# LayerNorm sums on one engine, conditioned values on ScalarE, and the last two channel groups regrouped, in a one-core streaming encoder layer

## The chip, the core and the metric
The kernel runs on one core of a Trainium2 chip. A core has five engines that run their own instruction streams and meet only at semaphores: TensorE (PE, matmuls; PEld is its weight load), VectorE (DVE), ScalarE (ACT), GpSimd (POOL) and SyncE (SP, which here only issues DMAs). The metric is the time of one execution in microseconds, given as the median of three runs.

## The reference, cut to what matters
One layer for 1,056 frames (1,024 of a prompt and 32 of a running stream, laid side by side), 1,024 channels:

```
out  = merged @ w_out                                # token-mixing sub-layer, before this: attention and mLSTM
x    = LayerNorm(alpha*x + gate1*out) * ln1_w + ln1_b          # the first LayerNorm, "LN1"
h    = x*(1+scale2) + shift2
u    = h @ w_up + b_up                               # 1024 -> 5632
uc   = conv_b + causal conv of width 3 over frames(u)
a, g = split(uc)                                     # 2816 each
x    = LayerNorm(alpha*x + gate2*((a*gelu(g)) @ w_down)) * ln2_w + ln2_b   # the second, "LN2"
```

All of it is float32. Each matmul operand is split into a rounded part (hi) and a remainder (lo), and three products (hi*hi, hi*lo, lo*hi) are summed, so that a 128 x 352 output tile over 1,024 channels takes 24 matmuls.

## The kernel before
Channels lie on the 128 partitions, in KT = 8 tiles (index m or k); frames lie along the free axis in NT = 3 blocks of 352 (index n). The third block holds the end of the prompt and the other stream, so an instruction with per-stream constants is issued in two pieces there (320 and 32). x lives in `x_c` (XC), the matmul input in `x_hilo_a` (XA).

Weights come as 512 KB panels, in one list whose order `ffn_panels()` writes out. SP loads them into two buffers; POOL splits each into hi and lo (`split`, L366 a cast and L368 a subtraction) and puts it into a ring of three slots (`w_hilo`). A panel may be written when the panel three places ahead of it in the ring has been used up by PE. The last panels have a place of their own (`w_tail_hilo`).

PE works through PSUM banks, eight of them, in an order that `bank_fills()` writes out and that PE's code repeats: a `fill` waits until the bank's former tile has been read.

The stages that the change touches:

- **LN1.** For each block n, PE makes the eight tiles of `merged @ w_out` (`out_tile`, L668). DVE adds each into x (`out_take`, L1467). Two running sums over the eight tiles are kept in `ln_sums`: the plain sum by POOL (`ln_sum`, L377), and the sum of squares, squared by ACT (L1089) and added by DVE (`ln_add_square`, L1476). After the third tile of the next block PE multiplies both sums by a matrix of 1/1024 (`ln_means`, L677 and L680, which wait for the semaphores of the two sums). DVE and ACT make the variance, its root and the shift (`ln_var`, `ln_sqrt`, `ln_shift`), and DVE normalises two tiles at a time (`ln_pair`, L1494 and L1496). Then h of each tile is made twice: rounded by ACT (`h2_high`, L1104) and in full by DVE (`h2_value`, L1502); POOL subtracts (`h2_low`, L385). PE's first up projection of a block waits for `h2_low`.
- **The channel sub-layer.** 11 groups j (FG = FF = 11). Each has four up panels ("u", j, 0..3), with three 24-matmul tiles each (`up`, L691), and two down panels ("d", j, 0..1), with twelve 6-matmul tiles each (`down`, L701). ACT moves an up tile out of PSUM (`up_take`, L1114) and begins the convolution (`up_tap`, L1121); DVE adds the two other taps (`conv_first` L1543, `conv_second` L1546); ACT takes the gelu (L1125), DVE multiplies (`ffn_prod`, L1556), ACT rounds (`ffn_round`, L1130), DVE makes the remainder (`ffn_low`, L1561 and L1562). PE runs the down tiles of group j-1 between the up tiles of group j, and DVE adds them into x (`down_take`, L1569).
- **The last groups.** The second half of the third last group's down tiles (FG-3, m = 4..7) comes after the up tiles of the last group. The last two groups have no down tiles of their own: for each (m, n) their products are summed in one bank (`down_last`, key "t", twelve matmuls), n by n.
- **LN2.** As LN1, on the "t" tiles; DVE takes a tile, adds a square, and normalises pairs of the block before; ACT scales pairs (L1175) and SP stores them. Behind the last tile stand both sums, PE's two means, the variance, the root, four pairs and the last store.

## Time and profile before
| | us |
|---|---|
| median of 3 runs (lowest, highest) | 2039.43 (2037.89, 2040.49) |
| profiled execution: its own time | 2039.05 |
| profiled execution: span from first to last instruction | 2037.2 |
| PE busy | 1946.1 (96%) |
| DVE busy | 1062.0 (52%) |
| ACT busy | 604.4 (30%) |
| POOL busy | 592.1 (29%) |

Between 1265 and 1903 us PE has no idle time at all; the stages above lie at 1121 to 1265 us (LN1 and the first up tiles) and at 1903 us to the end (the last groups and LN2). In a row of the timeline the first number is the start, the second the time from there to the end of the last instruction of the row, "xN" their count, and the bracket at the end the idle time of that engine just before and what ended it.

### The profile page before, as it was taken

To read this page: it belongs to the slowest core of one execution; us is meant where nothing else is said; L and a number is where in the kernel's file an instruction comes from. 1 tells how busy PE (TensorE), PEld (TensorE's weight loads), DVE (VectorE), ACT (ScalarE), POOL (GpSimd) and SP (SyncE) were. 2 spreads that over 40 slices of the span, in tenths; PEclk is the share of its full clock that TensorE was granted. 3 is DMA by queue.
4 is the path that set the end of the run, shared out by engine and by line. 5 is a ranking of instruction groups with operands and counts; after the bars stand their busy time and mean duration, and the time that the engine had idled before them with its cause. 6 is when DMAs were issued, how large, how long until landed. Compare 5 with 4: busy or idle time off the path is not lost.

```text
span 2037.2 us, 29596 instructions
## 1 busy us (share of the span) xinstructions
PE 1946.1 (96%) x11919; PEld 1845.6 (91%) x11919; DVE 1062.0 (52%) x1907; ACT 604.4 (30%) x1377; POOL 592.1 (29%) x354
## 2 busy tenths in 40 slices
PE   8889999999999999999899999999999999999983
PEld 6889888888799999989899998999999999999982
DVE  2797454344543333554434399554445445554577
ACT  1102444444223232333311134322222222322323
POOL 2332111121222222222233764323233332323321
PEclk9999999999999999999999999999999999999986
DMA  7562111111223332225533300111111111111102
GB/s 306 205 197 89 65 48 58 43 64 43 86 84 126 98 123 95 95 90 190 179 120 127 98 11 32 43 51 42 52 42 52 42 52 43 43 51 42 53 11 77
DMA packets 74183, 171.39 MB, mean 84 GB/s; under 512 B 8496, under 2 KB 37680, under 8 KB 73920
## 3 DMA queue, kind: packets, MB, share of 16 engines
q1 hardware_dynamic: 27168, 91.50, 13.3%
q10 hardware_dynamic: 46880, 78.02, 11.4%
q8 instruction: 94, 1.54, 0.3%
q14 instruction: 41, 0.34, 0.1%
HBM read 137.27 MB, written 32.22 MB: 83 GB/s over the span
## 4 chain that ended last, share of the span: by engine, by line
PE 82%; DVE 11%; DVEq 2%; ACT 2%; issue 1%; ACTq 1%; DMA 1%; POOL 0%; POOLq 0%
PE acc L421 30%; PE px L691 16%; PE acc L691 9%; PE px L701 7%; PE acc L701 4%; DVE adaT_tmp L1236 4%; PE px L484 2%; PE px L505 2%; PE px L503 2%; PE px L446 2%; PE px L668 1%; DVE x_c L1496 1%; DVE ln_sums L1476 1%; PE px L585 1%; DVEq L1495 1%
## 5 line engine op out<-in xcount | busy, mean ns | idle before, releaser
L421 PE MATMUL acc<-x_hilo_a,w_hilo 128*128 128x352 f32 x4176 | 727.5, 329 | 20.7 <-ACT x_c L799 10.0
L421 PEld LDWEIGHTS acc<-x_hilo_a,w_hilo 128*128 128x128 f32 x4176 | 674.3, 190 | 39.6 <-issue 28.9
L366 POOL CAST w_hilo<-w_raw 128x1024 fp32r<-128x1024 f32 x134 | 147.6, 1101 | 1299.2 <-PE acc L421 785.5
L368 POOL TENSOR_TENSOR w_hilo<-w_raw,w_hilo 128x1024 fp32r<-128x1024 f32 x134 | 343.5, 2563 | 10.7
L691 PE MATMUL px<-x_hilo_a,w_hilo 128*128 128x352 f32 x2016 | 326.9, 322 | 0.0
L691 PEld LDWEIGHTS px<-x_hilo_a,w_hilo 128*128 128x128 f32 x2016 | 323.0, 188 | 0.5 <-issue 0.5
L691 PE MATMUL acc<-x_hilo_a,w_hilo 128*128 128x352 f32 x1152 | 186.4, 321 | 0.0
L691 PEld LDWEIGHTS acc<-x_hilo_a,w_hilo 128*128 128x128 f32 x1152 | 183.8, 188 | 0.0
L701 PE MATMUL px<-ffn_act,w_hilo 128*128 128x352 f32 x888 | 151.0, 323 | 0.0
L701 PEld LDWEIGHTS px<-ffn_act,w_hilo 128*128 128x128 f32 x888 | 144.1, 189 | 0.2
L1569 DVE SCALAR_TENSOR_TENSOR x_c<-px,mod,x_c 128x352 f32<-128x352 f32 (+1 forms) x198 | 87.9, 483 | 68.6 <-PE px L701 68.4
L1114 ACT ACTIVATE u_rows<-px,ffn_consts 128x352 f32<-128x352 f32 (+2 forms) x113 | 50.7, 477 | 221.8 <-PE px L691 221.8
L1540 DVE COPY conv_out<-u_rows 128x2 f32<-128x2 f32 x44 | 16.1, 365 | 157.2 <-ACTq L1119 157.1
L1236 DVE CUSTOM_DVE_ANT_0 adaT_tmp<-adaT_ring,silu_bc 128x1024 f32<-128x1024 f32 x64 | 93.8, 1503 | 5.1 <-issue 4.2
L1543 DVE SCALAR_TENSOR_TENSOR stage<-u_rows,ffn_consts,stage 128x1058 f32<-128x1058 f32 x44 | 85.1, 1933 | 21.3 <-ACT stage L1121 21.3
L701 PE MATMUL acc<-ffn_act,w_hilo 128*128 128x352 f32 x552 | 95.7, 324 | 0.0
L868 ACT ACTIVATE stage<-acc 128x352 f32<-128x352 f32 x123 | 54.9, 457 | 129.6 <-PE acc L421 112.6
L701 PEld LDWEIGHTS acc<-ffn_act,w_hilo 128*128 128x128 f32 x552 | 90.0, 190 | 0.5 <-issue 0.5
L1569 DVE SCALAR_TENSOR_TENSOR x_c<-acc,mod,x_c 128x352 f32<-128x352 f32 (+2 forms) x122 | 55.0, 486 | 62.2 <-PE acc L701 62.0
L421 PE MATMUL acc<-x_hilo_b,w_hilo 128*128 128x352 f32 x504 | 80.4, 321 | 0.5 <-DVE stage L1453 0.5
L421 PEld LDWEIGHTS acc<-x_hilo_b,w_hilo 128*128 128x128 f32 x504 | 80.1, 188 | 0.7 <-issue 0.7
L1114 ACT ACTIVATE u_rows<-acc,ffn_consts 128x352 f32<-128x352 f32 (+2 forms) x63 | 28.8, 482 | 158.4 <-PE acc L691 158.4
(227 smaller groups left out, 2319.3 us busy)
## 6 DMA issues: line engine op xcount, KB each, us to landing
w_raw<-in_w_panels SPq DMA_DIRECT2D x142, 512.0 KB, 3.7
z_spill<-stage ACTq DMA_DIRECT2D x41, 528.0 KB, 2.7
adaT_ring<-in_w_adaT ACTq DMA_DIRECT2D x32, 512.0 KB, 4.4
stage<-z_spill ACTq DMA_DIRECT2D x20, 528.0 KB, 4.6
ada_ring<-in_w_ada SPq DMA_DIRECT2D x16, 512.0 KB, 9.4
zc<-z_spill ACTq DMA_DIRECT2D x8, 1024.0 KB, 7.6
x_c<-in_x SPq DMA_DIRECT2D x8, 528.0 KB, 10.2
x_c<-in_x ACTq DMA_DIRECT2D x8, 528.0 KB, 3.8
```

Source lines behind the costliest of these rows:

```text
L366: nc.gpsimd.tensor_copy(to[:, 0, :], raw[:, s, :]).then_inc(w_hi, 1)
L368: nc.gpsimd.tensor_tensor(to[:, 1, :], raw[:, s, :], to[:, 0, :].bitcast(F32), ALU.subtract).then_inc(w_ready, 1)
L421: last = mm(acc[:, n, 0:NW], whl[:, slot, wi, k * P:(k + 1) * P], rhs[:, xi, k, n * NW:(n + 1) * NW], start=(k == 0 and j == 0), stop=(k = ...
L446: last = mm(px[0:2, 3, i * P:(i + 1) * P], silu[:, 1, k, :], ada[:, q % KT, k * P:(k + 1) * P], start=(k == 0), stop=(k == KT - 1))
L484: last = mm(px[:, j // 2, (j % 2) * BAND:(j % 2) * BAND + w], qs[:, par, 4 * g + j, :], ks[:, par, g, 0:w], start=True, stop=True, skip_gr ...
L691: last = mm(to, w[:, wi, k * P:(k + 1) * P], XA[:, xi, k, n * NW:(n + 1) * NW], start=(k == 0 and q == 0), stop=(k == KT - 1 and q == 2))
L701: done = mm(to, w[:, wi, col:col + P], act[:, xi, k, n * NW:(n + 1) * NW], start=(first and k == 0 and q == 0), stop=(last and k == 1 and ...
L868: A(ST[:, slot, n * NW:(n + 1) * NW], acc[:, n, 0:NW], ACT.Copy).then_inc(acc_free[n], 1)
L1114: last = A(ub[:, i, 2 + a + 2 * s:2 + b + 2 * s], src[:, a - n * NW:b - n * NW], ACT.Identity, bias=fc[:, j, i, 0:1])
L1236: V.tensor_tensor_reduce(adaT_tmp[:, s, :], adaT[:, i, :], sbc[:, s, :], 1.0, 0.0, ALU.mult, ALU.add, ast[:, i, s:s + 1])
L1543: V.scalar_tensor_tensor(ST[:, i, 0:CW], ub[:, i, 0:CW], fc[:, j, i, 1:2], ST[:, i, 0:CW], ALU.mult, ALU.add)
L1569: last = V.scalar_tensor_tensor(XC[:, m, a:b], src[:, a - n * NW:b - n * NW], mod[:, 5, m, s:s + 1], XC[:, m, a:b], ALU.mult, ALU.add)
```

## The change
1. The plain sums move from POOL to DVE: `ln_add` follows each `out_take` and each "t" take. POOL's `ln_sum` is gone.
2. h in full is made by ACT, just before the rounded one (`h2_high` now issues both); DVE's `h2_value` is gone.
3. The split of the third up panel, which stood behind the second sum of the last block, now stands behind the eight `h2_low` of the first block.
4. The third last group's down tiles all run inside the loop; the up tiles of the last group follow without down tiles among them; then come the "t" tiles. In block n = 0 PE first opens all eight banks and runs the six matmuls of group FG-2 for all m, then the six of group FG-1 for all m. Blocks 1 and 2 are as before. One panel instead of two has its own place.
5. Small reorderings: both gelus ahead of both roundings in ACT's code (so far gelu, rounding, gelu, rounding), both products ahead of both remainders in DVE's; the signal for the conv state's store comes after the last remainder.

```
-    last = order.pop()
-    order += [("u", FF - 1, i) for i in range(4)]
-    return order + [last] + [("d", j, s) for j in (FF - 2, FF - 1) for s in range(2)]
+    order += [("u", j, i) for j in range(FF - TAIL + 1, FF) for i in range(4)]
+    return order + [("d", j, s) for j in range(FF - TAIL, FF) for s in range(2)]
...
-            for m in range(1, KT):
-                ln_sum(0, m, 0)
-            for n in range(1, NT):
-                for m in range(1, KT):
-                    ln_sum(0, m, n)
-                    if m == 2 and n == NT - 1:
-                        split(P_FFN + 2)
-                    if 3 <= m < KT - 1:
-                        for k in (2 * m - 6, 2 * m - 5):
-                            h2_low(n - 1, k)
-            for k in range(KT):
-                h2_low(NT - 1, k)
+            for n in range(NT):
+                for k in range(KT):
+                    h2_low(n, k)
+                if n == 0:
+                    split(P_FFN + 2)
...
-            for m in range(4, KT):
-                for n in range(NT):
-                    down(FG - 3, m, n)
-            for n in range(NT):
+            open_banks = [fill(("t", m, 0)) for m in range(KT)]
+            for m in range(KT):
+                down_last(open_banks[m], m, 0, range(FG - TAIL, FG - 1))
+            for m in range(KT):
+                down_last(open_banks[m], m, 0, range(FG - 1, FG))
+            for n in range(1, NT):
                 for m in range(KT):
-                    down_last(m, n)
+                    down_last(fill(("t", m, n)), m, n, range(FG - TAIL, FG))
...
             def h2_high(n, k):
+                q = n * KT + k
                 act.wait_ge(ln_t, n * KT // 2 + k // 2 + 1)
+                wait(act, h2_lo, q - 5)
+                for a, b, s in pieces(n):
+                    A(hslot(q)[:, a - n * NW:b - n * NW], XC[:, k, a:b], ACT.Identity, scale=der[:, s, k:k + 1],
+                      bias=der[:, 2 + s, k:k + 1])
...
+            def ln_add(ln, m, n):
+                cols = slice(n * NW, (n + 1) * NW)
+                V.tensor_tensor(lsum[:, 0, cols], XC[:, 0, cols] if m == 1 else lsum[:, 0, cols], XC[:, m, cols], ALU.add).then_inc(s1_add, 1)
...
                     down_take(("t", m, n))
+                    if m:
+                        ln_add(1, m, n)
                     if m > 1:
                         ln_add_square(1, m - 1, n)
```

One middle tile of LN1 on DVE (block 1, m = 4), before:

```order
L1467 SCALAR_TENSOR_TENSOR x_c<-px,mod,x_c 128x352
L1476 TENSOR_TENSOR ln_sums<-ln_sums,stage 128x352
L1494 TENSOR_TENSOR x_c<-x_c,ln_rstd 128x2x352
L1496 TENSOR_TENSOR x_c<-x_c,ln_shift 128x2x352
L1502 TENSOR_SCALAR stage<-x_c,der 128x352 x2
```

The same tile now (take, plain sum, sum of squares, pair):

```order
L1453 SCALAR_TENSOR_TENSOR x_c<-px,mod,x_c 128x352
L1486 TENSOR_TENSOR ln_sums<-ln_sums,x_c 128x352
L1462 TENSOR_TENSOR ln_sums<-ln_sums,stage 128x352
L1480 TENSOR_TENSOR x_c<-x_c,ln_rstd 128x2x352
L1482 TENSOR_TENSOR x_c<-x_c,ln_shift 128x2x352
```

The two values of h have left DVE, and one sum has come in between the take and the sum of squares.

POOL in LN1, from the end of block 1 to the middle of block 2, before (L377 is the plain sum, L385 `h2_low`, L366 and L368 the split of the third up panel):

```order
L385 TENSOR_TENSOR x_hilo_a<-stage,x_hilo_a 128x352 x2
L377 TENSOR_TENSOR ln_sums<-ln_sums,x_c 128x352
L377 TENSOR_TENSOR ln_sums<-x_c 128x352
L377 TENSOR_TENSOR ln_sums<-ln_sums,x_c 128x352
L366 CAST w_hilo<-w_raw 128x1024
L368 TENSOR_TENSOR w_hilo<-w_raw,w_hilo 128x1024
L377 TENSOR_TENSOR ln_sums<-ln_sums,x_c 128x352
```

All of POOL's work in LN1 now:

```order
L375 TENSOR_TENSOR x_hilo_a<-stage,x_hilo_a 128x352 x8
L365 CAST w_hilo<-w_raw 128x1024
L367 TENSOR_TENSOR w_hilo<-w_raw,w_hilo 128x1024
L375 TENSOR_TENSOR x_hilo_a<-stage,x_hilo_a 128x352 x16
```

Only remainders of h and one split are left; the split comes at once after the eighth remainder of block 0.

PE from the last up tiles on, before (L691 up tiles, L701 down tiles; acc and px are PSUM banks):

```order
L691 MATMUL px<-x_hilo_a,w_hilo 128x352 x72
L701 MATMUL px<-ffn_act,w_hilo 128x352 x12
L701 MATMUL acc<-ffn_act,w_hilo 128x352 x18
L701 MATMUL px<-ffn_act,w_hilo 128x352 x30
L701 MATMUL acc<-ffn_act,w_hilo 128x352 x18
L701 MATMUL acc<-ffn_act_tail,w_tail_hilo 128x352 x6
L701 MATMUL px<-ffn_act,w_hilo 128x352 x6
```

PE from the last up tiles on, now (L670 up tiles, L680 down tiles):

```order
L670 MATMUL acc<-x_hilo_a,w_hilo 128x352 x48
L680 MATMUL acc<-ffn_act,w_hilo 128x352 x6
L680 MATMUL px<-ffn_act,w_hilo 128x352 x30
L680 MATMUL acc<-ffn_act,w_hilo 128x352 x12
L680 MATMUL acc<-ffn_act_tail,w_hilo 128x352 x6
L680 MATMUL px<-ffn_act_tail,w_hilo 128x352 x18
L680 MATMUL px<-ffn_act_tail,w_tail_hilo 128x352 x12
L680 MATMUL acc<-ffn_act_tail,w_tail_hilo 128x352 x12
```

Before, 78 matmuls (72 of group FG-3 and the first 6 of FG-2) stood between the last up tile and the first use of the last group's activations (`ffn_act_tail`); now 48 do, all of group FG-2.

## Rows read from the trace of the kernel before
**Rows 1.** Who waited for whom, PE: total us, times, longest.
```profile
PE px L677 <- POOL ln_sums L377: 25.6, 4, 12.0
```
**Rows 2.** Timeline of LN1 around the two means with a wait, PE and DVE.
```profile
1197.02 0.83 PE L677 MATMUL px<-ln_sums,ones 128*128 128x352 f32 x2 [1.80 <-POOL ln_sums L377]
...
1224.08 0.70 DVE L1467 SCALAR_TENSOR_TENSOR x_c<-px,mod,x_c 128x320 f32<-128x320 f32 x2
...
1227.14 1.51 PE L677 MATMUL px<-ln_sums,ones 128*128 128x352 f32 x2 [5.80 <-POOL ln_sums L377]
...
1229.11 5.99 PE L691 MATMUL px<-x_hilo_a,w_hilo 128*128 128x352 f32 x24
```
**Rows 3.** Timeline of LN1, one tile (block 1, m = 4), DVE and POOL.
```profile
1178.23 0.58 DVE L1467 SCALAR_TENSOR_TENSOR x_c<-px,mod,x_c 128x352 f32<-128x352 f32 x1
...
1178.95 0.56 DVE L1476 TENSOR_TENSOR ln_sums<-ln_sums,stage 128x352 f32<-128x352 f32 x1
1179.43 1.63 DVE L1494 TENSOR_TENSOR x_c<-x_c,ln_rstd 128x704 f32<-128x704 f32 x1
1180.27 1.59 POOL L377 TENSOR_TENSOR ln_sums<-ln_sums,x_c 128x352 f32<-128x352 f32 x1
...
1182.70 0.84 DVE L1502 TENSOR_SCALAR stage<-x_c,der 128x352 f32<-128x352 f32 x2
```
**Rows 4.** Timeline of LN1, ACT: rounded h, two tiles each, blocks 0 and 2.
```profile
1177.07 1.26 ACT L1104 ACTIVATE x_hilo_a<-x_c,der 128x352 fp32r<-128x352 f32 x2 [3.29 <-DVE x_c L1496]
...
1236.40 1.81 ACT L1104 ACTIVATE x_hilo_a<-x_c,der 128x320 fp32r<-128x320 f32 x4 [2.00 <-DVE x_c L1496]
```
**Rows 5.** Chain of work that ended last: start, us, 72 matmuls at full clock.
```profile
1903.39 11.45 PE acc L691 x72
```
**Rows 6.** Timeline from the last up tile to the first use of its activations.
```profile
1926.32 0.71 ACT L1114 ACTIVATE u_rows<-px,ffn_consts 128x320 f32<-128x320 f32 x2 [3.26 <-PE px L691]
...
1928.44 2.62 DVE L1543 SCALAR_TENSOR_TENSOR stage<-u_rows,ffn_consts,stage 128x1058 f32<-128x1058 f32 x1 [0.90 <-ACT stage L1121]
...
1932.05 2.39 POOL L368 TENSOR_TENSOR w_tail_hilo<-w_raw,w_tail_hilo 128x1024 fp32r<-128x1024 f32 x1
...
1932.76 2.80 DVE L1546 SCALAR_TENSOR_TENSOR stage<-u_rows,ffn_consts,stage 128x1058 f32<-128x1058 f32 x1
...
1937.31 2.73 DVE L1556 TENSOR_TENSOR stage<-stage 128x1058 f32<-128x1058 f32 x1
...
1942.26 1.26 DVE L1556 TENSOR_TENSOR stage<-stage 128x1058 f32<-128x1058 f32 x1 [0.62 <-ACT stage L1125]
...
1943.56 1.06 ACT L1130 ACTIVATE ffn_act_tail<-stage 128x1024 fp32r<-128x1024 f32 x1 [1.33 <-DVE stage L1556]
...
1946.27 1.22 DVE L1561 TENSOR_TENSOR ffn_act_tail<-stage,ffn_act_tail 128x1024 fp32r<-128x1024 f32 x1
...
1947.64 2.12 PE L701 MATMUL acc<-ffn_act_tail,w_tail_hilo 128*128 128x352 f32 x6 [8.93 <-DVE ffn_act_tail L1562]
```
**Rows 7.** Timeline of LN2, DVE: block 1's start, block 2's end.
```profile
1967.65 0.53 DVE L1476 TENSOR_TENSOR ln_sums<-ln_sums,stage 128x352 f32<-128x352 f32 x1
...
1970.54 0.58 DVE L1569 SCALAR_TENSOR_TENSOR x_c<-px,mod,x_c 128x352 f32<-128x352 f32 x1 [1.32 <-PE px L701]
...
2012.63 0.70 DVE L1569 SCALAR_TENSOR_TENSOR x_c<-px,mod,x_c 128x320 f32<-128x320 f32 x2
2013.47 1.30 DVE L1476 TENSOR_TENSOR ln_sums<-ln_sums,stage 128x352 f32<-128x352 f32 x1
2014.69 0.88 DVE L1494 TENSOR_TENSOR x_c<-x_c,ln_rstd 128x704 f32<-128x704 f32 x1
...
2016.45 0.71 DVE L1569 SCALAR_TENSOR_TENSOR x_c<-px,mod,x_c 128x320 f32<-128x320 f32 x2
...
2021.14 0.52 DVE L1481 TENSOR_TENSOR ln_var<-px,ln_rstd 128x352 f32<-128x352 f32 x1 [1.94 <-PE px L680]
```
**Rows 8.** Stretches: us, PE, PEld, DVE, ACT, POOL busy (count), PEclk, DMA.
```profile
1947.60:1953.00 5.40, 5.36 (x18) 5.36 (x19) 0.58 (x1) 0.50 (x1) 0.00 (x0) 0.50 0.00 0
```

More of the change, by code:

```diff
@@ L60 @@
 NSLOT = 3
+TAIL = 2
 def ffn_panels():
     order = [("u", 0, i) for i in range(4)]
-    for j in range(1, FF - 1):
+    for j in range(1, FF - TAIL + 1):
         order += [("u", j, 0), ("u", j, 1), ("d", j - 1, 0), ("u", j, 2), ("u", j, 3), ("d", j - 1, 1)]
-    last = order.pop()
-    order += [("u", FF - 1, i) for i in range(4)]
-    return order + [last] + [("d", j, s) for j in (FF - 2, FF - 1) for s in range(2)]
+    order += [("u", j, i) for j in range(FF - TAIL + 1, FF) for i in range(4)]
+    return order + [("d", j, s) for j in range(FF - TAIL, FF) for s in range(2)]
 PANEL = {key: P_FFN + q for q, key in enumerate(ffn_panels())}
@@ L75 @@
 WO_PANELS = range(P_OUT + 2, P_OUT + KT)
-TAIL_PANELS = range(N_PANEL - 2, N_PANEL)
+TAIL_PANELS = range(N_PANEL - 2 * TAIL + NSLOT, N_PANEL)
 RING = [p for p in range(N_PANEL) if p not in WO_PANELS and p not in TAIL_PANELS]
@@ L95, in bank_fills @@
             order += [("u", j, i, n) for i in (2 * h, 2 * h + 1) for n in range(NT)]
-            if 2 * j + h < 2 * FF - 3:
+            if j <= FF - TAIL:
                 order += [("d", j - 1, m, n) for m in range(4 * h, 4 * h + 4) for n in range(NT)]
-    order += [("d", FF - 3, m, n) for m in range(4, KT) for n in range(NT)]
     for n in range(NT):
@@ L370, in split @@
                 pool.sem_inc(raw_used, 1)
-            def ln_sum(ln, m, n):
-                pool.wait_ge(r_rdy, rank(ln, m, n) + 1)
-                done = (KT - 1) * (NT * ln + n) + m - 1
-                wait(pool, s1_add, done)
-                cols = slice(n * NW, (n + 1) * NW)
-                nc.gpsimd.tensor_tensor(lsum[:, 0, cols], XC[:, 0, cols] if m == 1 else lsum[:, 0, cols], XC[:, m, cols], ALU.add)\
-                  .then_inc(s1_add, 1)
             def h2_low(n, k):
@@ L711, in down, with down_last @@
                 down_part(to, j, m, n, True, True).then_inc(ready(("d", j, m, n))[0], 1)
-            def down_last(m, n):
-                to = fill(("t", m, n))
-                for j in (FG - 2, FG - 1):
+            def down_last(to, m, n, groups):
+                for j in groups:
                     if n == 0 and m == 0:
@@ L719, in down_last @@
                         pe.wait_ge(w_ready, PANEL["d", j, m // 4] + 1)
-                    done = down_part(to, j, m, n, j == FG - 2, j == FG - 1)
-                done.then_inc(ready(("t", m, n))[0], 1)
+                    done = down_part(to, j, m, n, j == FG - TAIL, j == FG - 1)
+                if groups[-1] == FG - 1:
+                    done.then_inc(ready(("t", m, n))[0], 1)
             first = [fill(("o", 0, n)) for n in range(NT)]
@@ L757, in _ @@
                                 down(j - 1, m, n)
-            for m in range(4, KT):
-                for n in range(NT):
-                    down(FG - 3, m, n)
-            for n in range(NT):
+            open_banks = [fill(("t", m, 0)) for m in range(KT)]
[4 more added lines that the diff above has]
+            for n in range(1, NT):
                 for m in range(KT):
-                    down_last(m, n)
-                    if m == 2 and n:
+                    down_last(fill(("t", m, n)), m, n, range(FG - TAIL, FG))
+                    if m == 2:
                         ln_means(1, n - 1)
@@ L1496, in ln_pair @@
                 V.tensor_tensor(pair, pair, ln_c[:, n % 2:n % 2 + 1, :].to_broadcast([P, 2, NW]), ALU.add).then_inc(ln_t, 1)
-            def h2_value(n, k):
-                q = n * KT + k
-                wait(dve, h2_lo, q - 5)
-                for a, b, s in pieces(n):
-                    last = V.tensor_scalar(hslot(q)[:, a - n * NW:b - n * NW], XC[:, k, a:b], der[:, s, k:k + 1],
-                                           der[:, 2 + s, k:k + 1], ALU.mult, ALU.add)
-                last.then_inc(h2_d, 1)
-            def h2_pair(n, k):
-                ln_pair(n, k)
-                dve.drain()
-                h2_value(n, k)
-                h2_value(n, k + 1)
+            def ln_add(ln, m, n):
+                cols = slice(n * NW, (n + 1) * NW)
+                V.tensor_tensor(lsum[:, 0, cols], XC[:, 0, cols] if m == 1 else lsum[:, 0, cols], XC[:, m, cols], ALU.add).then_inc(s1_add, 1)
             for n in range(NT):
@@ L1531, in _ @@
             for k in range(0, KT, 2):
-                h2_pair(2, k)
+                ln_pair(2, k)
             dve.wait_ge(h2_hi, NT * KT)
-            dve.wait_ge(h2_d, NT * KT)
+            dve.drain()
             for k in range(KT):
@@ L1585, in _ @@
                 ffn_prod(0, t)
+            for t in range(2):
                 ffn_low(0, t)
-            for j in range(1, FG - 1):
+            for j in range(1, FG - TAIL + 1):
                 ffn_conv(j, 0)
```

47 lines of the change are left out of this document (16 added, 31 removed).

## The prediction
> **What bounds the kernel now.** I read the list of who waited for whom first, for PE. PE is busy 96% of the span, so only the places where it waits, and the work behind its last matmul, can give time back. The largest entry after the start of the kernel is the mean of LN1 and LN2, held up by POOL's plain sum: 25.6 us in four waits [rows 1]. Then the timeline around each. In LN1 the two waits are 1.80 and 5.80 us [rows 2], and nothing but DVE's pace is behind them: DVE's last take of block 2 starts at 1224.08, while PE had been done long before. The third place is the last group: 8.93 us for its activations [rows 6]. After that DVE sets the pace to the end: the longest of the four waits, 12.0, is PE's at the very last mean [rows 1]. So there are three stages to price: LN1, the last group, LN2.
>
> The reason for DVE's pace stands in rows 3 and 7. A sum of squares (L1476) takes 0.53 us when POOL is idle and 1.30 when POOL's sum starts beside it [rows 7]; the first half of a pair (L1494) takes 0.88 alone [rows 7] and 1.63 beside POOL [rows 3]; POOL's sum itself is stretched to 1.59 beside DVE [rows 3]. The stretch is each time about what the other needed. So a POOL instruction and a DVE instruction that reads two operands from SBUF run one after the other, and POOL's sum costs DVE about 0.78 us (1.30 less 0.53). The Trainium skill (SBUF — State Buffer, "Who interferes with whom") says the same as a rule: with two SBUF inputs VectorE takes the pair of ports that it shares with GpSimd, and whoever comes first keeps it for the whole instruction. It makes the price of a POOL sum the whole of POOL's instruction, not a share; these rows agree.
>
> **LN1.** Removed from DVE per tile in the steady part (m = 4 to 6): two values of h, 0.84, and POOL's plain sum as a neighbour, 0.78. Added: one sum, 0.48 from one start to the next (L1476 to L1494 in rows 3). But two POOL subtractions per tile remain, and now they begin later. Before, the cycle of a tile is 5.2 us (1178.23 to 1182.70 plus 0.84, rows 3). Now: take 0.72 (1178.23 to 1178.95), two sums 0.48 each: 1.7. POOL's first subtraction is released by two ACT activations (1.26, rows 4), so at about 1.4; it gets in after the second sum and, at some 0.85, holds DVE to 2.5. First half of the pair to 3.4; the second subtraction, released at 2.6, gets in next, to 4.2; second half to 5.0 at most, the next take a little before: I take 4.8. That saves 0.4 per tile, three times per block. In the tile m = 3, which has no subtraction beside it, the saving is 0.84 + 0.78 - 0.48 = 1.1. Together 2.3 per block. With a small gain in the tile before, I take 2.4, so the last take of block 2 starts near 1221.7.
>
> Block 1's saving does not carry into block 2: the moved split now falls on block 2's first sums, and a split's subtraction is 2.39 long [rows 6]; before, it lay beside the reciprocal, which POOL did not disturb. The wait of 1.80 goes, but DVE enters block 2's tile m = 3 as late as before.
>
> After the last take of block 2 (0.83 with two pieces) the plain sum is done at +1.3. The sum of squares is now later than the plain sum: ACT has four activations for the last pair (2 x 1.26) ahead of its square (0.5), and a subtraction of POOL and the addition follow: +4.1. PE resumes the up tiles at 1221.7 + 4.1 + 0.5 = 1226.3 instead of 1229.11: **2.8 us earlier**.
>
> Block 2 of h must then keep up. ACT's two tiles take 1.81 before [rows 4], 3.62 now. From the first up tile after the means, the first pair begins at +7.3 (1236.40 less 1229.11, rows 2 and 4), four pairs add 14.5, three evictions between them about 1.4 (estimated at one activation of 0.45 each), POOL about 1: +24.2. PE needs the last at five tiles of 3.82 (a third of rows 5), 2.2 more for the first at half clock (5.99, rows 2), and 7/8 of a tile: +24.6. It just fits; were the clock full, PE would gain 2.2 and wait 1.8. Bounds of LN1: if the two subtractions and ACT's doubled work keep the old cycle and h is late, a loss of 1; if neither holds DVE, a gain of 5 (cycle 3.7, all of the first wait).
>
> **The last group.** 72 down matmuls move ahead of the last up tiles: these end 11.45 us later [rows 5]. From ACT's eviction of the last up tile to PE's use of the activations it was 21.3 us (1926.32 to 1947.64, rows 6). In between DVE had twelve takes of the third last group, and POOL three splits; now no take, and two splits. By rows 6, from the eviction: first tap's start at +2.1 and its end at +4.7 as before, beside the first split; then the cast of the second split (about 0.9) and the second tap (1.1 of its 2.80, the rest was blocking): +6.8. The second split's subtraction gets in next (2.39): +9.2, then the first product (1.1): +10.3; second product, 1.2 more: +11.5; its rounding 1.2 (1943.56 to the start of its last small piece and that piece): +12.7; the two remainders 1.37 each, the second behind the first: **+14.1**. So PE resumes 11.45 - 7.2 = 4.25 later than now. PE's cover is shorter, 48 matmuls (7.6 us) behind the wait for eight free banks (until the last eviction is over, 0.71), so it still idles about 6 us and still starts at half clock, 0.50 granted after the wait [rows 8], 2.12 for the first six matmuls [rows 6].
>
> The rule of the skill speaks against the change here, since the two splits that are left fall on the convolution of the last group alone. That is in the 14.1; without any blocking the same chain is 10.1 (2.1 + 1.3 + 1.4 + 1.3 + 1.3 + 1.2 + 1.5), and with none of the blocking gone and only the takes gone (12 at some 0.4) 16.4.
>
> **LN2, counted from PE's resumption.** Nothing is left on POOL here, so no sum is blocked. Block 0: before, each tile took PE twelve matmuls, 1.91, and block 1's first take came at 1966.94 (0.71 before the first of rows 7), 19.3 after the resumption. Now half of these matmuls are done before, and DVE sets the pace: first take at +2.1, then two tiles at half-clock pace (about 1.8 each), and tiles of take 0.71 and two sums 0.44 each, 1.6: block 0 ends at +15.1, **4.2 saved**. Blocks 1 and 2, up to the last take at 2016.45 [rows 7], 49.5 us: eleven of thirteen sums of squares were blocked and lose 0.78 each (-8.6; the cycle of 3.82 from 2012.63 to 2016.45 holds one), thirteen plain sums come in at 0.44 (+5.7), and the waits for PE at the block's start go, one of them 1.32 [rows 7]: **3.9 saved**. From the last take to the variance it was 4.69 (2016.45 to 2021.14): the plain sum no longer waits for POOL, and PE's first mean starts earlier: **0.5 saved**. Behind it nothing changes.
>
> **The sum.** LN1 -2.8, last group +4.25, LN2 -4.2 - 3.9 - 0.5: -7.1. The profiled execution took 2039.05 (span 2037.2 and 1.85 around it), so 2031.9; the median of before, 0.38 higher, would give 2032.3. I forecast **2032**. At nothing I cost the reordering of gelus, products and remainders in groups 0 to 9: PE has no idle time there, and a group's remainders are needed some 30 us after its last up tile, behind the next group's two up panels.
>
> **Rivals.**
> - *LN1 gives nothing back.* ACT and POOL's subtractions become the pace where POOL's sums were: 5.80 stays. For it: only 0.4 per tile was found. Against: 0.84 per tile leaves DVE for certain. Then 2039.05 - 4.3 = 2034.7 (2034 to 2036.5).
> - *The cover is lost and eats the gain.* The chain of the last group stays at 21.3, each DVE step waiting for POOL and ACT as before, so PE resumes 11.45 later instead of 4.25: 2032 + 7.2 = 2039 (2036.5 to 2043). For it: two splits start just when the last up tile ends. Against: one split and twelve takes are gone, and the takes stand in rows 6 as the gaps between the taps and the products.
> - *DVE is the bound and gets more work: slower.* If 1.30 were the own price of a sum of squares in LN2 (waiting for ACT's square, not for POOL), no blocking would go, and 0.44 per added sum would stand alone: in blocks 1 and 2 +5.7 less the 1.8 of waits, block 0 about +1, the last group +4.25, LN1 -1.4 (0.48 - 0.84 per tile): +7.6, so 2047. It decides from the point where L1476 in LN2 stays above 0.9. Against: the same instruction takes 0.53 where POOL rests.
> - *More than forecast.* The last group's chain at 10.1: 2028.
>
> **How the numbers follow.** A median of three tells 0.2% (4.1 us) from no change: faster means under 2035.4, slower over 2043.5. Chances: forecast (2028.5 to 2035.4) 0.54; LN1 gives nothing 0.18, half of it under 2035.4; cover lost 0.15, 0.13 of it within 0.2% and 0.01 beyond either end; slower 0.07; more 0.06. Faster 0.54 + 0.09 + 0.06 + 0.01 = 0.70, slower 0.08, same 0.22. The range leaves out a tenth on either side: 2026.5 at the lower end (LN1's bound of 5 or the chain at 10.1, and a little of the other), 2037.5 at the upper (LN1 at nothing and the chain at 16.4 give 2037).
>
> **What would show it.** In the profile after: L1476's successor (sum of squares) at 0.53 in all of LN2 and the plain sum at the same; the DVE cycle of a tile in LN1 4.8, in LN2 3.4; PE's wait at the first mean of LN1 gone, at the second about 3.6 before the plain mean and 2 before the squares; PE's wait for the last group's activations about 6, ended 14 us after the last up tile's eviction; last take 60 to 61 us after that. Wrong: a sum of squares over 0.9 in LN2, an LN1 cycle of 5.2 or more, a wait of PE for `h2_low` in block 2 over 2 us, or a chain of 16 us and more behind the last up tile.

## The result

The changed kernel takes 2030.07 us, the median of six runs (2028.93 to 2031.47); the kernel before, timed beside it, 2039.96 (2037.77 to 2045.10). The ratio is 0.9950, with a 95% interval of 0.9937 to 0.9963: about 10 us faster, more than twice the 0.2% (4.1 us) that the prediction took as what can be told from no change. The profiled execution took 2029.85 us, its span 2028.1. DVE's busy time hardly moved (1062.0 to 1056.2 us), POOL's fell by 39 and ACT's rose by 17.

Who PE waited for now (total us, times, longest):

```profile
PE px L656 <- DVE ln_sums L1486: 19.6, 3, 11.0
...
PE acc L680 <- DVE ffn_act_tail L1539: 5.0, 1, 5.0
...
PE px L659 <- DVE ln_sums L1462: 1.7, 1, 1.7
...
```

The mean's 25.6 us in four waits [rows 1] are 19.6 in three, and it is DVE's own sum (L1486) that ends them; the 8.93 for the last group's activations [rows 6] are 5.0. The new entry of 1.7 is the wait for the sum of squares that was foreseen.

The timeline of PE at LN1's means in the changed kernel (start, us, bracket: wait before and releaser):

```profile
1194.79 0.75 PE L656 MATMUL px<-ln_sums,ones 128*128 128x352 f32 x2
...
1222.13 0.83 PE L656 MATMUL px<-ln_sums,ones 128*128 128x352 f32 x2 [2.80 <-DVE ln_sums L1486]
...
1224.66 1.51 PE L659 MATMUL px<-ln_sums,ones 128*128 128x352 f32 x2 [1.70 <-DVE ln_sums L1462]
...
1225.45 5.32 PE L670 MATMUL px<-x_hilo_a,w_hilo 128*128 128x352 f32 x24
```

The first wait is gone and the second is 4.5 in two parts where it was 5.80; the up tile behind it starts 3.66 earlier than in [rows 2], of which 0.29 was there before LN1 began (its first out tile started at 1120.67 instead of 1120.96). One tile of LN1 (block 1, m = 5) and the moved split, DVE and POOL, same timeline:

```profile
1181.20 0.57 DVE L1453 SCALAR_TENSOR_TENSOR x_c<-acc,mod,x_c 128x352 f32<-128x352 f32 x1
...
1181.91 0.53 DVE L1486 TENSOR_TENSOR ln_sums<-ln_sums,x_c 128x352 f32<-128x352 f32 x1
1182.36 0.52 DVE L1462 TENSOR_TENSOR ln_sums<-ln_sums,stage 128x352 f32<-128x352 f32 x1
...
1182.65 2.60 POOL L375 TENSOR_TENSOR x_hilo_a<-stage,x_hilo_a 128x352 fp32r<-128x352 f32 x2 [2.12 <-ACT x_hilo_a L1090]
1182.79 1.64 DVE L1480 TENSOR_TENSOR x_c<-x_c,ln_rstd 128x704 f32<-128x704 f32 x1
...
1184.51 1.48 DVE L1482 TENSOR_TENSOR x_c<-x_c,ln_shift 128x704 f32<-128x704 f32 x1
...
1185.92 0.57 DVE L1453 SCALAR_TENSOR_TENSOR x_c<-acc,mod,x_c 128x352 f32<-128x352 f32 x1
...
1195.73 2.39 POOL L367 TENSOR_TENSOR w_hilo<-w_raw,w_hilo 128x1024 fp32r<-128x1024 f32 x1
...
1195.90 2.60 DVE L1486 TENSOR_TENSOR ln_sums<-ln_sums,x_c 128x352 f32<-128x352 f32 x1
```

From take to take it is 4.72, as against 5.2 in [rows 3]. An instruction is called blocked here when it takes longer than alone because the other engine is at work. Both halves of the pair are still blocked (1.64 and 1.48, alone 0.88 and 0.89), now both by POOL's subtractions; before, the first half was behind a subtraction (POOL's L385, from 1178.09 on, two in 2.22) and the second behind the plain sum, which starts at 1180.27 [rows 3]. The last two rows are the split on block 2's first sums: a sum of 0.53 takes 2.60.

The last group in the changed kernel, ACT, DVE, POOL and PE, answering to [rows 6]:

```profile
1933.47 0.71 ACT L1100 ACTIVATE u_rows<-acc,ffn_consts 128x320 f32<-128x320 f32 x2 [3.26 <-PE acc L670]
...
1935.60 2.63 DVE L1520 SCALAR_TENSOR_TENSOR stage<-u_rows,ffn_consts,stage 128x1058 f32<-128x1058 f32 x1 [0.90 <-ACT stage L1107]
...
1937.34 1.79 POOL L365 CAST w_tail_hilo<-w_raw 128x1024 fp32r<-128x1024 f32 x1 [0.23 <-POOL w_hilo L367]
1938.30 1.94 DVE L1523 SCALAR_TENSOR_TENSOR stage<-u_rows,ffn_consts,stage 128x1058 f32<-128x1058 f32 x1
1939.21 3.30 POOL L367 TENSOR_TENSOR w_tail_hilo<-w_raw,w_tail_hilo 128x1024 fp32r<-128x1024 f32 x1
1940.17 4.64 DVE L1533 TENSOR_TENSOR stage<-stage 128x1058 f32<-128x1058 f32 x2
...
1947.49 2.13 PE L680 MATMUL acc<-ffn_act_tail,w_hilo 128*128 128x352 f32 x6 [4.99 <-DVE ffn_act_tail L1539]
```

From the eviction to PE's resumption it is 14.02 where it was 21.32, and PE resumes at almost the same moment as before. LN2, DVE, grouped by form from 1940 us on (count | busy us, mean ns of one), answering to the sums of [rows 7]:

```profile
L1462 DVE TENSOR_TENSOR ln_sums<-ln_sums,stage 128x352 f32<-128x352 f32 x21 | 10.9, 520 | 0.4
L1486 DVE TENSOR_TENSOR ln_sums<-ln_sums,x_c 128x352 f32<-128x352 f32 x18 | 9.5, 526 | 2.4
```

And its ends in the timeline, DVE: block 1's first take, the last two takes and the variance.

```profile
1962.14 0.58 DVE L1546 SCALAR_TENSOR_TENSOR x_c<-acc,mod,x_c 128x352 f32<-128x352 f32 x1
...
2004.52 0.70 DVE L1546 SCALAR_TENSOR_TENSOR x_c<-px,mod,x_c 128x320 f32<-128x320 f32 x2
...
2008.00 0.70 DVE L1546 SCALAR_TENSOR_TENSOR x_c<-px,mod,x_c 128x320 f32<-128x320 f32 x2
...
2012.31 0.53 DVE L1467 TENSOR_TENSOR ln_var<-px,ln_rstd 128x352 f32<-128x352 f32 x1 [1.89 <-PE px L659]
```

All 21 sums of squares are at 0.52, a tile takes 3.48 (2004.52 to 2008.00; 3.82 before), block 1 begins 14.65 after PE's resumption (19.3 before), the last take comes 60.51 after it (68.81 before).

### The profile page after: what moved, and what is told of

Read it like the earlier page. It is cut to its first block, busy times and chain, and to the rows that moved or that the text cites. A ratio compares the mean times of both kernels' runs of the same rounds, so it can differ in the third digit from the quotient of the medians.

```text
span 2028.1 us, 29540 instructions
## 1 busy us (share of the span) xinstructions
PE 1944.3 (96%) x11919; PEld 1843.8 (91%) x11919; DVE 1056.2 (52%) x1917; ACT 621.4 (31%) x1409; POOL 552.8 (27%) x312
## 4 chain that ended last, share of the span: by engine, by line
PE 83%; DVE 10%; ACT 2%; DVEq 2%; issue 1%; ACTq 1%; DMA 1%
PE acc L400 30%; PE px L670 15%; PE acc L670 9%; PE px L680 6%; DVE adaT_tmp L1222 4%; PE acc L680 4%; PE px L647 2%; PE px L463 2%; PE px L484 2%; PE px L482 2%; PE px L425 2%; PE acc L647 1%; PE px L564 1%; PE px L566 1%; PE px L565 1%
## 5 line engine op out<-in xcount | busy, mean ns | idle before, releaser
L367 POOL TENSOR_TENSOR w_hilo<-w_raw,w_hilo 128x1024 fp32r<-128x1024 f32 x135 | 349.1, 2586 | 10.8
L670 PE MATMUL px<-x_hilo_a,w_hilo 128*128 128x352 f32 x1992 | 322.5, 322 | 0.0
L670 PEld LDWEIGHTS px<-x_hilo_a,w_hilo 128*128 128x128 f32 x1992 | 318.6, 188 | 0.5 <-issue 0.5
L670 PE MATMUL acc<-x_hilo_a,w_hilo 128*128 128x352 f32 x1176 | 190.4, 321 | 0.0
L670 PEld LDWEIGHTS acc<-x_hilo_a,w_hilo 128*128 128x128 f32 x1176 | 187.6, 188 | 0.0
L680 PE MATMUL px<-ffn_act,w_hilo 128*128 128x352 f32 x894 | 150.5, 322 | 0.0
L680 PEld LDWEIGHTS px<-ffn_act,w_hilo 128*128 128x128 f32 x894 | 144.1, 188 | 0.2
L680 PE MATMUL acc<-ffn_act,w_hilo 128*128 128x352 f32 x546 | 94.4, 324 | 1.1 <-ACT u_rows L1100 1.1
L680 PEld LDWEIGHTS acc<-ffn_act,w_hilo 128*128 128x128 f32 x546 | 88.6, 189 | 1.9 <-issue 1.9
```

The costliest lines, as they stand in the source:

```text
L367: nc.gpsimd.tensor_tensor(to[:, 1, :], raw[:, s, :], to[:, 0, :].bitcast(F32), ALU.subtract).then_inc(w_ready, 1)
L670: last = mm(to, w[:, wi, k * P:(k + 1) * P], XA[:, xi, k, n * NW:(n + 1) * NW], start=(k == 0 and q == 0), stop=(k == KT - 1 and q == 2))
L680: done = mm(to, w[:, wi, col:col + P], act[:, xi, k, n * NW:(n + 1) * NW], start=(first and k == 0 and q == 0), stop=(last and k == 1 and ...
```

## The experiments

The time of one kernel scatters by some 3 us either way; its stages scatter less. So every run is read by three stretches of its profile. **A**: from the first out tile to the up tile behind LN1's second mean. **B**: from there to PE's resumption with the last group's activations. **C**: from there to PE's last mean of a plain sum. Each is a difference of two starts in PE's timeline. The kernel before has A 108.15, B 718.53, C 70.71; the changed kernel 104.78, 722.04, 62.02. Four kernels that leave LN1 as in the changed kernel have A within 104.79 to 104.82. But two that leave it as before have 108.15 and 108.39, and two that make h on ACT and the plain sums on POOL have 103.06 and 104.01, though LN1's second mean starts equally late in them, 102.06 and 102.05 after the first out tile (in the other pair it differs by 0.25). Here are these means, first h on ACT, then "mixed" (PE):

```profile
1222.58 0.83 PE L676 MATMUL px<-ln_sums,ones 128*128 128x352 f32 x2 [3.42 <-POOL ln_sums L377]
```

```profile
1222.18 1.51 PE L672 MATMUL px<-ln_sums,ones 128*128 128x352 f32 x2 [3.40 <-POOL ln_sums L377]
```

Behind the same wait one mean ran at 0.83 and the other at 1.51; the granted clock was 0.88 over the 2.5 us from 1222 in the first, 0.50 over the 3 us from 1222 in the second. So A holds up to 1 us of PE's clock behind its wait, and a difference in A of less than that is read only together with the start of the mean. Between runs the first out tile itself starts anywhere from 1119.5 to 1124.2, in stages that no kernel here touches. That adds to the scatter of the times; how much of it this is, and its cause, were not looked for. Each ratio in the table is to the kernel before timed beside that run (medians 2038.20 to 2041.48), so medians of different rows are compared by their ratios.

| kernel | median us (n) | ratio to before | A | B | C |
|---|---|---|---|---|---|
| sums on VectorE alone | 2038.36 (10) | 0.9989 (0.9979 to 0.9999) | 111.08 | 718.02 | 66.54 |
| h on ScalarE alone | 2033.88 (10) | 0.9973 (0.9963 to 0.9982) | 103.06 | 718.36 | 71.06 |
| both | 2031.04 (4) | 0.9953 (0.9939 to 0.9968) | 104.79 | 717.96 | 67.58 |
| last groups alone | 2038.22 (10) | 0.9991 (0.9978 to 1.0004) | 108.39 | 722.24 | 63.04 |
| changed, POOL reads in LN2 | 2047.24 (4) | 1.0044 (1.0031 to 1.0058) | 104.82 | 722.29 | 77.72 |
| changed, POOL writes in LN2 | 2030.30 (4) | 0.9960 (0.9947 to 0.9974) | 104.79 | 722.04 | 62.03 |
| changed, tail split late | 2029.71 (5) | 0.9956 (0.9944 to 0.9969) | 104.82 | 720.62 | 61.37 |
| changed, up split late | 2031.40 (5) | 0.9956 (0.9942 to 0.9970) | 103.08 | 723.42 | 62.59 |
| three edits | 2023.46 (4) | 0.9915 (0.9898 to 0.9932) | 101.56 | 720.06 | 60.86 |
| mixed, tail split late | 2025.63 (5) | 0.9936 (0.9923 to 0.9950) | 104.01 | 719.80 | 61.35 |

### The parts one by one

**The sums on VectorE alone** (part 1 of the change, on the kernel before):

```
-                    ln_sum(0, m, n)              # POOL, and the same for LN2
...
                     out_take(m, n)
+                    ln_add(0, m, n)              # DVE, and the same behind the "t" takes
```

> The kernel before with the plain LayerNorm sums alone moved from POOL to DVE (values of h stay on DVE, the last groups as before). Theory (a POOL instruction and a DVE instruction with two SBUF operands run one after the other; POOL's sum costs DVE 0.78 us, the sum on DVE 0.44): every sum of squares in LN2 takes 0.53 instead of 1.30; blocks 1 and 2 of LN2 3 us shorter, block 0 unchanged because PE's twelve matmuls per tile set its pace, the end 0.4 shorter, LN1 about 1 shorter (tile cycle 5.0 instead of 5.2). Together -4.5 us. Rival (the gain came from the regrouping, and sums on DVE only add work): +6 us or more, with the sum of squares still near 1.3.

Measured: about 2 us less in the medians, not 4.5. C fell by 4.2, a little more than foreseen (3.4), but A rose by 2.9 where a gain of 1 was expected. The sums are worth something in LN2 and cost in LN1. Where, the timeline of this kernel shows, from a tile of block 1 (m = 6) to behind LN1's first mean (DVE, POOL, PE):

```profile
1191.50 1.26 DVE L1461 TENSOR_TENSOR ln_sums<-ln_sums,stage 128x352 f32<-128x352 f32 x1
...
1198.83 2.50 POOL L368 TENSOR_TENSOR w_hilo<-w_raw,w_hilo 128x1024 fp32r<-128x1024 f32 x1
1199.05 2.66 DVE L1461 TENSOR_TENSOR ln_sums<-ln_sums,stage 128x352 f32<-128x352 f32 x1
...
1201.85 1.51 PE L665 MATMUL px<-ln_sums,ones 128*128 128x352 f32 x2 [3.83 <-DVE ln_sums L1461]
...
1202.64 6.69 PE L653 MATMUL px<-x_hilo_a,w_out_hilo 128*128 128x352 f32 x24
...
1209.44 0.71 DVE L1452 SCALAR_TENSOR_TENSOR x_c<-px,mod,x_c 128x320 f32<-128x320 f32 x2 [2.36 <-PE px L653]
```

POOL, without its sums, reaches the split early, and the split falls on the sum for which the mean waits. The wait goes on to cost clock: the out tile behind it takes 6.69 where it took 4.26 before (granted 0.58 from 1202 to 1209, and 1.00 from 1198 to 1202.2 before), and DVE then waits 2.36 for that tile. So this take comes 4.4 later after the first out tile than before (86.3 and 81.9); the tiles behind it win 1.4 back by the mean. In the tile itself only the sum of squares is blocked (1.26); the two halves of the pair take 0.88 and 0.89, where both were blocked before. With the sum that DVE now makes itself, the tile takes 5.08, as against 5.2.

**The values of h on ScalarE alone** (part 2):

```
             def h2_high(n, k):
+                for a, b, s in pieces(n):
+                    A(hslot(q)[:, a - n * NW:b - n * NW], XC[:, k, a:b], ACT.Identity, scale=der[:, s, k:k + 1], ...
...
-                h2_value(n, k); h2_value(n, k + 1)      # DVE, behind each pair
```

> The kernel before with the full values of h alone made by ACT. Theory: DVE loses 0.84 per tile in LN1, but POOL's three instructions per tile (two subtractions, one sum) and DVE's three (sum of squares, two halves of a pair) still take turns, 3 x 0.85 + 2.3 and the take: cycle stays at 5.0 to 5.4, so LN1 gains 0 to 1 us, LN2 nothing: -0.5 us in all. Rival (DVE's own work sets LN1's pace): cycle 4.4, LN1 2.5 to 3 us shorter by this part alone.

Measured: A fell by 5.1, so the rival held, and by more than it said. Of the 5.1, 4.1 are there when the second mean starts (106.18 after the first out tile before, 102.06 here); the last 1.0 is PE's clock, since the two means ran at 1.51 and 1.38 before and at 0.83 and 0.76 here. One tile of LN1 in this kernel (block 1, m = 6), DVE and POOL:

```profile
1184.35 0.57 DVE L1471 SCALAR_TENSOR_TENSOR x_c<-acc,mod,x_c 128x352 f32<-128x352 f32 x1
...
1185.06 0.56 DVE L1480 TENSOR_TENSOR ln_sums<-ln_sums,stage 128x352 f32<-128x352 f32 x1
1185.20 1.23 POOL L377 TENSOR_TENSOR ln_sums<-ln_sums,x_c 128x352 f32<-128x352 f32 x1
1185.55 1.63 DVE L1498 TENSOR_TENSOR x_c<-x_c,ln_rstd 128x704 f32<-128x704 f32 x1
...
1186.39 3.16 POOL L384 TENSOR_TENSOR x_hilo_a<-stage,x_hilo_a 128x352 fp32r<-128x352 f32 x2
...
1187.25 1.48 DVE L1500 TENSOR_TENSOR x_c<-x_c,ln_shift 128x704 f32<-128x704 f32 x1
1188.66 0.57 DVE L1471 SCALAR_TENSOR_TENSOR x_c<-acc,mod,x_c 128x352 f32<-128x352 f32 x1
```

The tile takes 4.31. POOL has three instructions in it here, two in the changed kernel and three before, and DVE has two blocked instructions (0.75 and 0.6 too long) in all three. So beside h on ACT a POOL sum less did not spare DVE a blocked instruction, while with h still on DVE, in the run above, it spared one; POOL's third instruction finds room beside DVE's takes, which read PSUM and are not blocked (0.57 beside POOL). What is left of the difference between 4.31 and 4.72 is the sum that DVE makes itself, 0.44.

**Both, with the last groups as before:**

> The kernel before with both moves, the last groups as before. Theory: LN1 as in the changed kernel (up tile after the second mean 3.7 us earlier, the half-clock tile 0.6 shorter: -4.3 in all), the last group as before, LN2 shorter by 3 in blocks 1 and 2 and 0.4 at the end: -7.6 us, 1.5 to 2 short of the changed kernel. Rival (the regrouping brings the gain of LN2): -4.3 us, LN2 as long as before.

Measured: A 104.79, as in the changed kernel, so the sums take back 1.7 of what h alone had, or 0.8 by the A of the mixed kernel; C 3.1 less than before. What they take back is not at the plain mean, which starts 0.6 earlier than with h alone (101.47 and 102.06 after the first out tile), but at the mean of the squares, which waits 1.70 more. In total 9.4 us between the medians, and 7.1 by the three stretches, near the theory's 7.6. So in the whole change the regrouped last groups bring some 1.5 by the stretches (B 4.1 more, C 5.6 less), which the ratios (0.9953 and 0.9950) can't tell.

**The last groups alone** (parts 4 and 5, with sums and h as before):

```
-            for m in range(4, KT):
-                for n in range(NT):
-                    down(FG - 3, m, n)
+            open_banks = [fill(("t", m, 0)) for m in range(KT)]
+            ...                                   # FG-2 for all m, then FG-1 for all m
```

> The changed kernel with the sums back on POOL and the values of h back on DVE, so only the regrouped last groups and the small reorderings are left. Theory: PE resumes 4.25 us later after the last group; LN2's block 0 is no longer paced by PE but by DVE with blocked sums (0.71 + 1.24 per tile, 1.95): 2.8 us back, and the waits for PE at block 1's start go, 1.8: -0.4 us in all, no change that can be told. Rival (regrouping brings LN2's gain): -4 us or better.

Measured: B rose by 3.7, C fell by 7.7, 3.7 less over all three stretches, so it was the rival (-4) that held in LN2, and not the -0.4. The medians differ by 2.25, which the scatter of this kernel (2033.83 to 2045.77) doesn't let one tell from no change. The fall in C is larger than the 4.2 of block 0 in the prediction; POOL's sums are still there, yet block 0 is no slower for them. Timeline of this kernel, DVE and POOL, in block 0 of LN2:

```profile
1955.55 0.53 DVE L1479 TENSOR_TENSOR ln_sums<-ln_sums,stage 128x352 f32<-128x352 f32 x1
1955.67 7.16 POOL L377 TENSOR_TENSOR ln_sums<-ln_sums,x_c 128x352 f32<-128x352 f32 x6
```

Here DVE's sum comes first and POOL's waits: six POOL sums take 1.19 each, at DVE's pace, and DVE's stay at 0.53 to 0.57. In blocks 1 and 2, up to the last take, ten of DVE's sums are at 1.30 to 1.32, as many as before. In the kernel before POOL is idle when a take ends, starts its sum at once and comes first, and DVE pays 1.30 [rows 7]. So the price of a POOL sum is not a constant; it goes to the engine that comes second.

### The contention by itself

**A POOL instruction that reads, put back beside each sum of LN2:**

```
+            for n in range(NT):
+                for m in range(1, KT):
+                    pool.wait_ge(r_rdy, rank(1, m, n) + 1)
+                    wait(pool, dm, n * (KT - 1) + m - 1)
+                    nc.gpsimd.tensor_tensor(ST[:, 2, 0:NW], ST[:, 0, 0:NW], ST[:, 1, 0:NW], ALU.add).then_inc(dm, 1)
```

> The changed kernel, with one idle instruction per tile put back on POOL in LN2: beside each take of a last tile (m = 1 to 7) POOL adds two 352-wide SBUF tiles into a third that nobody uses. Nothing waits for it, so only contention can act. Theory (a POOL instruction that reads SBUF and a DVE instruction with two SBUF operands take turns): the plain sum or the sum of squares beside it goes from 0.53 us to about 1.3; 21 of them, about 14 of these in blocks 1 and 2 where DVE sets the pace: LN2 8 to 14 us longer, 2040 against 2030. Rival (the 1.30 of before was the wait for POOL's result or for ScalarE's square): every sum stays at 0.53 and the time within 1 us of the changed kernel.

Measured: C rose by 15.7 to 77.72, beyond the upper end of 14. DVE and POOL by form from 1940 us on:

```profile
L1493 DVE TENSOR_TENSOR ln_sums<-ln_sums,x_c 128x352 f32<-128x352 f32 x18 | 23.5, 1307 | 2.5
L1469 DVE TENSOR_TENSOR ln_sums<-ln_sums,stage 128x352 f32<-128x352 f32 x21 | 10.8, 514 | 0.4
```

```profile
L392 POOL TENSOR_TENSOR stage<-stage 128x352 f32<-128x352 f32 x21 | 19.7, 936 | 62.5 <-DVEq L1557 62.5
```

The plain sum that starts beside it takes 1.31 instead of 0.53, all 21 of them (the three that begin a block stand in a row of their own, at 1.30): 21 x 0.78 = 16.4. Block 0, which the expectation had spared, was not: its mean came 19.9 after PE's resumption, 15.4 in the changed kernel. The sum of squares right behind stays at 0.51. Nothing waits for this POOL instruction, so the 1.30 of [rows 7] needs no wait for ACT or for POOL's result.

**A POOL instruction that only writes** (`nc.gpsimd.memset(ST[:, 2, 0:NW], 0.0)` in its place):

> As the run with POOL's idle sum, but the idle instruction only fills its tile with zeros and reads nothing. Theory: what collides is POOL's reading together with DVE's second operand, so the sums stay at 0.53 us and the time stays within 1 us of the changed kernel (2030). Rival (any POOL instruction that touches SBUF blocks DVE): sums at 1.0 or more and 5 us or more.

Measured: C 62.03 against 62.02. The same views:

```profile
L1493 DVE TENSOR_TENSOR ln_sums<-ln_sums,x_c 128x352 f32<-128x352 f32 x18 | 9.5, 526 | 2.5
```

```profile
L392 POOL MEMSET stage<- 128x352 f32 x21 | 8.2, 393 | 58.5 <-DVEq L1557 58.5
```

The sums stay at 0.53, though the two overlap: one such write of POOL runs from 1961.80 to 1962.19, the sum beside it from 1961.83. The write is also shorter than the read (0.39 against 0.94); a read of 0.39 was not tried. The Trainium skill (SBUF — State Buffer, "Who interferes with whom") says just this: a VectorE instruction with two SBUF inputs collides with a GpSimd instruction that reads SBUF, and not with one that only writes. The two runs agree.

### What is left, and a faster version

**The split of the panel with its own place moved behind the last group's remainders:**

```
                 elif p in TAIL_PANELS:
                     pool.wait_ge(*ready(("u", FG - 1, 3, NT - 1)))
+                    pool.wait_ge(fa_lo, 2 * FG)
```

> The changed kernel, with the split of the panel with its own place moved behind the remainders of the last group, so that POOL disturbs that group's convolution with one split fewer. Theory: the cast and the subtraction of that split lie inside the chain from the last eviction to PE's resumption (14.0 us) and cost it 2.8: chain about 11.2, PE's wait 5.0 goes to about 2.2, total -2.8 us, 2027.2. Rival 1 (the two products and two remainders go one after the other behind ScalarE, POOL was hidden): chain stays at 13.5 to 14. Rival 2: the panel is now late, PE waits for it in block 0 of the last tiles (a wait of 1 us or more on the split), and the gain goes there.

Measured, timeline of the last group (ACT, DVE, PE, POOL):

```profile
1937.03 0.71 ACT L1101 ACTIVATE u_rows<-acc,ffn_consts 128x320 f32<-128x320 f32 x2 [3.26 <-PE acc L671]
...
1941.86 1.32 DVE L1524 SCALAR_TENSOR_TENSOR stage<-u_rows,ffn_consts,stage 128x1058 f32<-128x1058 f32 x1
...
1943.10 2.51 DVE L1534 TENSOR_TENSOR stage<-stage 128x1058 f32<-128x1058 f32 x2
...
1948.23 1.23 PE L681 MATMUL acc<-ffn_act_tail,w_hilo 128*128 128x352 f32 x6 [2.27 <-DVE ffn_act_tail L1540]
```

The chain is 11.20, and PE's wait 2.27, both as expected. The two products take 2.51 instead of 4.64 and the second tap 1.32 instead of 1.94. PE waits nowhere for the late panel, so rival 2 is out. The total hides it (2029.71; in the profiled execution, 2029.95, the first out tile was 2.1 later than in the changed kernel's); B fell by 1.4 and not by 2.8, because the up tile behind LN1's second mean took 6.72 at the low clock instead of 5.32.

**The split of the third up panel behind block 1's remainders** (`if n == 0:` becomes `if n == 1:`):

> The changed kernel, with the split of the third up panel behind the eight remainders of block 1 instead of block 0, so that it no longer lies on block 2's first sums. Theory: with its 2.4 us subtraction beside the first half of block 2's work DVE entered block 2 late; now DVE's takes of block 2 come about 2 us earlier against the first out tile, PE's two waits at the second mean (2.80 and 1.70) shrink by 1.8 to 2.5 in sum, total about 2028. Rival: block 2's pace is set by the pair tiles and POOL's remainders, which the split now lies beside: the waits move by under 0.7, or POOL's remainders of block 1 end later and the up tiles of block 2 wait for them.

Measured: A fell by 1.7, and of the two waits at the second mean the first (PE's timeline):

```profile
1223.91 0.83 PE L656 MATMUL px<-ln_sums,ones 128*128 128x352 f32 x2 [1.09 <-DVE ln_sums L1486]
...
1226.44 1.51 PE L659 MATMUL px<-ln_sums,ones 128*128 128x352 f32 x2 [1.70 <-DVE ln_sums L1462]
```

2.80 became 1.09, just short of the theory's lower end. A is 103.08, and with h on ACT and no sum on DVE it was 103.06 and 104.01: with this split out of the way, the sums on DVE cost LN1 nothing that can be told. The total did not show it: the up tile behind took 6.69 at the low clock, and the first out tile started 3.5 later than in the changed kernel.

**Three edits**: both late splits, and ACT's square of the last tile ahead of the activations for the last pair but one.

```
                 for m in range(3, KT - 1):
                     ln_square(0, m, n)
+                    if m == KT - 2:
+                        ln_square(0, KT - 1, n)
                     for k in (2 * m - 6, 2 * m - 5):
                         h2_high(n - 1, k)
-                ln_square(0, KT - 1, n)
```

> The changed kernel with three edits: the late split of the up panel as above, the late split of the panel of the last groups (which shortened the chain from the last eviction to PE's resumption from 14.0 to 11.2), and ScalarE's square of the last tile of blocks 1 and 2 issued ahead of the four activations for the last pair but one. Theory: second mean 2 us earlier by the first edit and the squares' own wait of 1.70 down to about 0.4 by the third; chain 11.2: 2030.1 - 2 - 1.3 - 2.8 = 2024, that is the same as the mixed version with POOL's sums in LN1 (2025.6) or a little better. Rival (the mean's wait is the plain sum's alone, the square only hides behind it): 2026 to 2027.

Measured: 2023.46 us (2022.85 to 2023.97), the lowest median and ratio of all, and faster than the changed kernel (the intervals of the ratios, 0.9898 to 0.9932 and 0.9937 to 0.9963, do not meet). PE's waits from 1100 us on:

```profile
PE px L657 <- DVE ln_sums L1488: 16.5, 3, 9.8
PE acc L681 <- DVE ffn_act_tail L1541: 2.3, 1, 2.3
PE px L671 <- POOL x_hilo_a L376: 1.3, 2, 0.9
...
```

At the second mean the waits are 1.10 and 0.22 and A is 3.2 less than in the changed kernel. The up tile behind runs at full clock, 4.27 instead of 5.32, and now block 2's remainders of h are a little late: 1.3, a new entry.

**Mixed**: h on ACT, the plain sums of LN1 back on POOL (as in the kernel before, with the split between them), those of LN2 on DVE, the last groups regrouped, and the late split of the tail.

> What the single parts point to: values of h on ScalarE, plain sums of LN1 back on POOL with the third up panel's split where it was, plain sums of LN2 on VectorE, the last groups regrouped, the late split of the run before. Theory (the gain in LN1 comes from h alone, POOL's sums there disturb VectorE less than VectorE's own sums cost it): up tile after LN1's second mean 1.7 us earlier than in the changed kernel, the last group as in the run with the late split, LN2 as in the changed kernel: 2030.1 - 1.7 - 2.8 = 2025.6. Rival (LN1's difference of 1.7 was scatter between executions): 2027.3.

Measured: 2025.63, the expected number; but by its stages partly for other reasons: A fell by 0.8 and not by 1.7 (in LN1 PE's mean waits 3.40 for POOL's sum, and the two means then ran at the low clock, 1.51 and 1.38 us). So the rival was half right: LN1 here is that of h on ACT, and 0.95 of what had been read there as the sums' price was PE's clock. By its median it lies between the changed kernel and the three edits, which keep the sums on DVE and take away what blocks them; its ratio's interval (0.9923 to 0.9950) meets those of both.

## Why the prediction was right

**The sum.** Foreseen -7.1, found -9.1 in the span; the sign, the order of the stages, and the mechanisms in the last group and LN2 were right. In LN1 the sum was near and its reason only partly right. By terms, from the profiles of before and after:

| step | foreseen | found |
|---|---|---|
| LN1, to the up tile behind the second mean | -2.8 | -3.4 (A) |
| last group: PE's resumption | +4.25 | +3.5 (B) |
| LN2, to the last take | -8.1 | -8.3 |
| last take to variance | -0.5 | -0.4 |
| ahead of LN1, and behind the variance | 0 | -0.3 and -0.3 |

**LN1** was mis-sized by 0.6: against the first out tile, DVE's last take of block 2 came 3.2 earlier than before, where 2.4 was foreseen. The tile was put at 4.8 and took 4.72; the first mean's wait went; the split did fall on block 2's first sums, with 2.60 for a sum. The second mean's waits were put at 3.6 and 2 and were 2.80 and 1.70. No wait for block 2's remainders came, as the sum had it, and the sentence on what would happen at full clock (a gain of 2.2, then a wait of 1.8) came near in the run with three edits: the tile took 4.27 instead of 5.99, 1.7 gained, and 1.3 waited. The rival "LN1 gives nothing back" is refuted by A.

**The step in LN1 that failed** is the reason given, not the sum: "POOL's plain sum as a neighbour, 0.78" was counted as removed per tile. The 0.78 was read in LN2; in LN1's tile before, the sum stood behind the first half of the pair and made the second 0.6 too long. The single parts show that its removal is worth no blocked instruction in the tile beside h on ACT (two in 4.31, two in 4.72), one with h on DVE, and that LN1's whole gain is the values of h (-5.1, of which 1.0 is clock; -4.1 in the mixed kernel), of which the sums take back 0.8 to 1.7. The prediction came out near partly by luck: it charged the two subtractions with what it had credited to the sum. Where I then split the change into parts, the error showed: -0.5 was expected from h alone.

**The last group.** The chain was put at 14.1 and is 14.02, with the steps as worked out: first tap blocked by the first split, the second tap and a product by the second. PE resumes 0.15 earlier than before; the 0.7 between +4.25 and +3.5 is the up tile after LN1 (5.99 to 5.32), which got the full clock back sooner; nothing in the prediction foresaw that. The rivals "cover lost" (21.3) and "more than forecast" (10.1) are refuted. With one of the two splits gone the chain was 11.20, still above the 10.1 that was worked out for no blocking at all.

**LN2.** Block 1 was put at 15.1 after the resumption and began at 14.65; the last take at 60.7 and came at 60.51. Blocks 1 and 2 were put at 3.9 and gave 3.65. The sum's parts hold a slip: in the timeline before ten of the thirteen sums of squares are blocked, not eleven, so it is -7.8 and not -8.6; with +5.7 and the 1.8 of waits that the rival "slower" names this gives the 3.9. The rival "slower" needed the 1.30 to be the sum's own price; the two idle POOL instructions decide against it. What the prediction did not see is that regrouping alone spares block 0 from blocking: with the regroup in place the sums' move is worth 1.0 in C (63.04 to 62.02), without it 4.2.

**The reorderings**, costed at nothing, show no wait: between 1265 and 1900 us PE is busy for 635.00 of 635.00 in both profiles. Whether they gain anything by themselves was not tried.

## What to carry to other kernels

Count the blocked instructions of a cycle in the timeline, not the instructions that could block: in these runs whoever came second paid, and POOL, where it had slack in the cycle, moved its work there. When a long split or copy on POOL has no near deadline, move it behind the short chain that others wait for; here two such moves and one earlier square were worth more than half of what the whole change brought. Read parts of a change by stage anchors within a profile, since totals scatter more than the parts are worth, and look at the clock before an anchor that stands behind a wait: here it moved one anchor by 1 us with nothing else changed.
